# One core, a fused two-block transformer in split fp32: groups of TensorE transposes issued two at a time

## The chip, the core and the metric

The kernel runs on one core of one Trainium2 chip. The time is the device time of one execution, in microseconds. The engines of the core run side by side and meet through semaphores: TensorE (PE), VectorE (DVE), ScalarE (ACT), GpSimd (POOL) and SyncE (SP), which issues the DMAs.

## What is computed

The reference takes 256 tokens of width 2048 through three layers, all in fp32, and each weight is used once:

```python
# layer 0: stick-breaking attention, then the residual update; layer 1: latent attention, same update
x = x + rms_norm(out, g_post)
x = x + (p_i @ w_pp) * sigmoid(x @ w_pg)
# shared keys/values of layer 1
ckv, k_rope = split(rms_norm(x, kv_norm) @ w_dkv)
# last layer: 16 meta tokens in front; gated linear attention and causal pooling, side by side
q, k, v, r, glr, pu = split(rmsnorm(h, norm1) @ w_in)
h = h + concat(gla(q, k, v, glr) * silu(r), pool(pu)) @ w_out
h = h + square(relu(rmsnorm(h, norm2) @ mlp_w1)) @ mlp_w2      # 2048 -> 8192 -> 2048
```

## The kernel before, in words

**Units.** Every product streams its weight through a ring of four slots of 128 x 1024 elements. SP loads a unit into `raw` (L358, L414), ACT copies it rounded into `whi` (L1016), DVE writes the rest `raw - whi` into `wlo` (L1494), and PE takes three matmuls for each tile: hi times hi, hi times lo, lo times hi (L485, L486, L487; L852 to L854 in the last layer's transposed products; L961 and L964 in the MLP's up products). A unit has two k tiles of 512 columns: 2 x 2 token tiles x 3 = 12 matmuls. A chunk is 8 units, 96 matmuls, and gives 512 output columns for both token tiles. The `ckv` stage is narrower, 288 columns for each matmul, and the stages `k2`, `v2` and `pu` have 272.

**Lead.** `along` on ACT and on DVE runs through a chunk unit by unit: first the split of the unit that is three ahead (ACT waits until PE has used the slot's last unit), then the hooks of that unit.

**Transposes.** Activations are produced token by token and must lie channel by channel as the next product's left operand. They are turned on PE against the identity, in batches (`batch`, L497) of four 128 x 128 transposes that fill one PSUM bank `tp[n % 2]`. ACT then takes the bank as the hi part (`hi_batch`, L1049 without a gain, L1052 with one, L1035 for `mixed`), DVE the lo part (`lo_batch`, L1523 and L1527) and frees the bank with `tp_done`. Batch n waits in `batch` until batch n - 2 is done. Batches are numbered in one global order, `BATCH`. Each activation of width 2048 has 8 groups: `ogA` and `ogB` (gated attention outputs), `x1` and `x3` (residuals into the gate products), `x2a`, `x2b`, `x4` (residuals into the next layer), `mixed`, `x5`. `ckv` and `cq` (latents) have two each, `qdec` (decayed queries) 2, `kend` (keys) 2, `vT` (values) 4.

**Hooks.** A plan such as `{1: [3], 2: [4]}` says: ahead of unit 1 turn group 3, ahead of unit 2 group 4. PE, ACT and DVE each follow the same plan in their own streams: `turns` on PE, `his` on ACT, `los` on DVE. With `need=name`, unit u of a product waits until group u of that name is done. Where a turned group isn't hooked to a unit it stands between two chunks, as `x1` in the `ple` stage (one unit a chunk) of `post`.

**Attention of layer 1.** The stage `attb` runs head pairs in slots `c` = 0 to 7. In the last slot its four units stand with `ogB` turned ahead of units k = 1, 2, 3; `turned(c)` (L715) transposes the probabilities ahead of the last unit, ACT copies them (L1300), `outputs(c)` (L722 to L724) multiplies with the values, and ACT's `silu_out` (L1156) frees the accumulators for `out_b`, whose first product waits for it (`gates_out`).

Of the kernel before, what the change touches and what calls it, by code (L numbers as in the profile page):

```python
# [143 lines left out]
def build(nc, w, const, out):  # L144
# [3 lines left out]
    with ctx:  # L148
# [306 lines left out]
        def _(pe):  # L455
# [215 lines left out]
            product(S["cq"], 0, ahi, alo, need="x2b", hooks=join(turns_staged("ckv", {4: [0], 5: [1]}, c + 1, c), {7: [turn_k_rope]}))  # L671
# [61 lines left out]
            for c in range(SLOTS):  # L733
                more = c + 1 < SLOTS
                for k, (query, uu) in enumerate(slot_units(c)):
                    if k == 0:
                        scores(c)
                        if c == 0:
                            evacuated(S["uv2"].c0 + 1)
                        elif c % 2 == 0:  # L740
                            pe.wait_ge(evac_act, gate_chunk_at(c // 2 - 1) + 1)
                    if not more and k:
                        turn("ogB", k - 1)
                    if query and uu == 0 and c:
# [12 lines left out]
                outputs(c)  # L757
# [78 lines left out]
            def columns(name, j, hooks={}):  # L836
# [5 lines left out]
                for uu in range(s.units):  # L842
# [61 lines left out]
            product(S["r2"], 1, x4hi, x4lo, hooks=join({6: [heads_out]}, turns("mixed", {6: [0], 7: [1]})))  # L904
# [100 lines left out]
        def _(act):  # L1005
# [179 lines left out]
            def post(layer, y, x1, x2, gain, norms):  # L1185
                s = S[f"out_{'ab'[layer]}"]
                for j in range(4):
                    p = (s.c0 + j) % 2
                    along(s, j, his(y, bhi, None, OG_LATE if layer == 0 else SPREAD) if j == 0 else {})
# [13 lines left out]
                for j in range(4):  # L1203
                    p = (s.c0 + j) % 2
                    split_to(s.u0 + j + 4)
                    if j:
                        hi_batch(x1, j - 1, ahi)
                    ended(s, j)
                    for t in range(TT):
                        m = act.activation(pp[:, t, j * CH:(j + 1) * CH], acc[p][t][:, :], ACT.Copy)  # L1210
                    m.then_inc(evac_act, 1)
                s = S[f"gate{layer}"]
                for j in range(4):
# [5 lines left out]
                    hooks = join({4: [last_squares]}, his(x2, x4hi if layer else bhi, gain, ALONG[j])) if j else his(x1, ahi, None, SPREAD)  # L1219
# [37 lines left out]
            along(s, 0, his("ckv", kvhi, GC["kvl"], {4: [0], 5: [1]}))  # L1257
# [33 lines left out]
            for c in range(SLOTS):  # L1291
                for query, uu in slot_units(c):
                    if uu % 4 == 3:
                        if c:
                            act.wait_ge(sem("attB_out"), c)
                        if c == SLOTS - 1:
                            hi_batch("ogB", 1, bhi)
# [5 lines left out]
                    if c == SLOTS - 1 and uu % 4 == 1:  # L1303
                        hi_batch("ogB", 0, bhi)
# [9 lines left out]
                if c == SLOTS - 1:  # L1314
                    hi_batch("ogB", 2, bhi)
# [86 lines left out]
            for j in range(2):  # L1402
                p = (s.c0 + j) % 2
                along(s, j, join({0: [lambda: hi_pooled(3)]}, his_mixed({6: [0], 7: [1]})) if j else
# [82 lines left out]
        def _(dve):  # L1487
# [178 lines left out]
            def post(layer, y, x1, x2, gain, norms):  # L1666
                s = S[f"out_{'ab'[layer]}"]
                for j in range(4):
                    p = (s.c0 + j) % 2
                    along(s, j, los(y, bhi, blo, None, OG_LATE if layer == 0 else SPREAD) if j == 0 else {})  # L1670
# [13 lines left out]
                for j in range(4):  # L1684
# [4 lines left out]
                    if j >= 1:  # L1689
                        lo_batch(x1, j - 1, ahi, alo)  # L1690
                    split_to(s.u0 + j + 4)
                s = S[f"gate{layer}"]
                for j in range(4):
                    c, p = s.c0 + j, (s.c0 + j) % 2
                    hooks = los(x2, x4hi if layer else bhi, x4lo if layer else blo, gain, ALONG[j]) if j else los(x1, ahi, alo, None, SPREAD)
# [32 lines left out]
            along(s, 0, join(los("ckv", kvhi, kvlo, GC["kvl"], {4: [0], 5: [1]}), {7: [k_rope_out]}))  # L1728
# [66 lines left out]
            for c in range(SLOTS):  # L1795
                more = c + 1 < SLOTS
                scores_out(c)
                for k, (query, uu) in enumerate(slot_units(c)):
# [11 lines left out]
                    if not more and k in (1, 2):  # L1810
                        lo_batch("ogB", k - 1, bhi, blo)
                outputs_over_sums(c)
                if c == SLOTS - 1:
                    lo_batch("ogB", 2, bhi, blo)
# [83 lines left out]
            for j, hooks in enumerate(({1: [keys_from_start], 3: [keys_to_end]},  # L1898
                                       {0: [lambda: decayed_queries_out(0)], 1: [lambda: decayed_queries_out(1)],
                                        2: [lambda: turned_out("kend", 0, kend[:, 0, :])], 3: [lambda: turned_out("kend", 1, kend[:, 1, :])]},  # L1900
                                       {1: [lambda: values_turned(0)], 3: [lambda: values_turned(1)]}, {1: [lambda: values_turned(2)]})):
                columns("v2", j, vT[:, 2 * j, :], vT[:, 2 * j + 1, :], sem("vT"), hooks)
# [65 lines left out]
            for j, hooks in enumerate(({1: [lambda: values_turned(3), lambda: turned_out("kvM", 0, kvM[:, :])], 3: [lambda: head_in(0)]},  # L1968
# [6 lines left out]
                                   los("mixed", ahi, alo, mixed_gain, {6: [0], 7: [1]})))  # L1975
# [191 lines left out]
```

## Time and profile before

| | |
|---|---|
| Median of 3 runs | 2110.72 us (2108.91, 2110.72, 2110.99) |
| The profiled execution's own time | 2112.99 us |
| Its span, first to last instruction | 2111.2 us |
| PE busy in the span | 2095.2 us, 99% |
| DVE, ACT, POOL busy | 1209.6, 1047.9, 111.3 us |
| Granted TensorE clock, mean | 0.998 |
| Moved by DMA | 375.09 MB, 178 GB/s |

Busy time is the union of an engine's instructions. On PE the matmuls are pipelined: one of 512 columns is shown some 0.39 us long, and the next starts 0.23 us after it, so on PE the starts count, not the lengths. In a timeline row "x4" after an instruction means four of that kind in a row, the time is that from the first's start to the last's end, and "[0.54 <-ACT stg L1156]" is idle time ahead of it with what ended that.

### The profile page before, as it was taken

How to read it: one execution, taken by the hardware profiler on the slowest of the kernel's cores; microseconds unless marked ns; L12 is line 12 of the kernel's file. 1: busy time of each engine (PE TensorE's matmuls, PEld its weight loads, DVE VectorE, ACT ScalarE, POOL GpSimd, SP SyncE). 2: the span in 40 equal slices, each digit the busy share in tenths (PEclk: the TensorE clock that was granted, in tenths of full speed). 3: DMA queues.
4: the chain of work that ended last, by engine and by line, in shares of the span. 5: the costliest groups of instructions: out<-in, count | busy, mean ns of one | idle time of the engine just before them, and what ended most of it. 6: DMA issues, size and time to landing. Idle time of an engine off the chain costs nothing.

```text
span 2111.2 us, 26739 instructions
## 1 busy us (share of the span) xinstructions
PE 2095.2 (99%) x10740; PEld 1784.2 (85%) x10740; DVE 1209.6 (57%) x1371; ACT 1047.9 (50%) x1400; POOL 111.3 (5%) x98
## 2 busy tenths in 40 slices
PE   9999999999999999999999999999999999999998
PEld 7888887888898888888889998888888888888887
DVE  5555555556666556556655557556555655655655
ACT  6443566645565455445555345554434434534443
POOL 0000334100000121000000000000000000000000
PEclk9999999999999999999999999999999999999999
DMA  7666544555555544555554546556566566566654
GB/s 255 183 186 188 170 150 147 171 192 188 181 161 182 153 149 135 171 185 191 184 163 140 145 135 200 185 176 193 193 192 189 190 196 188 188 196 190 188 191 149
DMA packets 209052, 375.09 MB, mean 178 GB/s; under 512 B 13844, under 2 KB 44790, under 8 KB 208535
## 3 DMA queue, kind: packets, MB, share of 16 engines
q1 hardware_dynamic: 208934, 373.46, 56.7%
q8 instruction: 82, 1.34, 0.3%
q14 instruction: 36, 0.29, 0.0%
HBM read 371.31 MB, written 2.10 MB: 177 GB/s over the span
## 4 chain that ended last, share of the span: by engine, by line
PE 96%; ACT 1%; POOL 1%; DVE 1%; issue 0%; DMA 0%; SPq 0%; ACTq 0%; POOLq 0%
PE acc L485 22%; PE acc L487 22%; PE acc L486 22%; PE acc L961 6%; PE xb L961 3%; PE tp L961 3%; PE tp L497 3%; PE acc L964 3%; PE acc L852 2%; PE acc L853 2%; PE acc L854 2%; PE tp L964 1%; PE xb L964 1%; PE tp L600 1%; PE xb L706 0%; PE xb L707 0%
## 5 line engine op out<-in xcount | busy, mean ns | idle before, releaser
L1494 DVE TENSOR_TENSOR wlo<-raw,whi 128x1024 fp32r<-128x1024 f32 (+2 forms) x706 | 865.2, 1228 | 770.6 <-ACT whi L1016 769.5
L1016 ACT ACTIVATE whi<-raw 128x1024 fp32r<-128x1024 f32 (+2 forms) x706 | 737.1, 1046 | 857.7 <-PE acc L487 616.1
L485 PE MATMUL acc<-whi,ahi 128*128 128x512 f32 x1552 | 614.3, 396 | 0.0
L487 PE MATMUL acc<-whi,alo 128*128 128x512 f32 x1552 | 605.3, 390 | 0.0
L486 PE MATMUL acc<-wlo,ahi 128*128 128x512 f32 x1552 | 604.5, 390 | 0.0
L487 PEld LDWEIGHTS acc<-whi,alo 128*128 128x128 f32 x1552 | 291.3, 188 | 61.6
L486 PEld LDWEIGHTS acc<-wlo,ahi 128*128 128x128 f32 x1552 | 291.8, 188 | 57.7
L485 PEld LDWEIGHTS acc<-whi,ahi 128*128 128x128 f32 x1552 | 291.6, 188 | 57.5
L961 PE MATMUL acc<-bT,whi 128*128 128x512 f32 x512 | 161.3, 396 | 1.1 <-DVE x L1993 0.7
L485 PE MATMUL acc<-whi,bhi 128*128 128x512 f32 (+1 forms) x320 | 120.4, 376 | 0.5 <-ACT stg L1156 0.5
L487 PE MATMUL acc<-whi,blo 128*128 128x512 f32 (+1 forms) x320 | 118.6, 371 | 0.0
L486 PE MATMUL acc<-wlo,bhi 128*128 128x512 f32 (+1 forms) x320 | 118.5, 370 | 0.0
L964 PEld LDWEIGHTS acc<-bT,wlo 128*128 128x128 f32 x512 | 96.2, 188 | 22.7
L964 PE MATMUL acc<-bT,wlo 128*128 128x256 f32 x512 | 100.6, 278 | 0.0
L852 PE MATMUL acc<-lhi,whi 128*128 128x272 f32 x320 | 93.9, 294 | 0.0
L853 PE MATMUL acc<-llo,whi 128*128 128x272 f32 x320 | 93.2, 291 | 0.0
L854 PE MATMUL acc<-lhi,wlo 128*128 128x272 f32 x320 | 92.9, 290 | 0.0
L961 PE MATMUL tp<-bT,whi 128*128 128x512 f32 x256 | 80.4, 395 | 0.0
L961 PE MATMUL xb<-bT,whi 128*128 128x512 f32 x256 | 80.4, 395 | 0.0
L961 PEld LDWEIGHTS acc<-bT,whi 128*128 128x128 f32 x512 | 78.2, 189 | 2.2 <-DVE x L2036 1.0
L485 PEld LDWEIGHTS acc<-whi,bhi 128*128 128x128 f32 x320 | 60.1, 188 | 10.5 <-ACT stg L1156 0.7
L487 PEld LDWEIGHTS acc<-whi,blo 128*128 128x128 f32 x320 | 60.1, 188 | 10.2
(323 smaller groups left out, 2256.6 us busy)
## 6 DMA issues: line engine op xcount, KB each, us to landing
raw<-in_mlp_w SPq DMA_DIRECT2D x256, 512.0 KB, 4.3
raw<-in_w_in_a SPq DMA_DIRECT2D x128, 512.0 KB, 3.8
raw<-in_w_ple_gate SPq DMA_DIRECT2D x64, 512.0 KB, 3.9
raw<-in_w_in SPq DMA_DIRECT2D x64, 512.0 KB, 3.8
raw<-in_w_in_b SPq DMA_DIRECT2D x40, 512.0 KB, 3.6
raw<-in_w_out_a SPq DMA_DIRECT2D x32, 512.0 KB, 4.3
raw<-in_w_out_b SPq DMA_DIRECT2D x32, 512.0 KB, 4.3
raw<-in_w_out SPq DMA_DIRECT2D x32, 512.0 KB, 4.2
```

Of the source, the lines that this page charges most:

```text
L485: pe.matmul(o, hi[:, kt, tok], whi[:, slot, wc], start=start, stop=False)
L486: pe.matmul(o, hi[:, kt, tok], wlo[:, slot, wc], start=False, stop=False)
L487: mm = pe.matmul(o, lo[:, kt, tok], whi[:, slot, wc], start=False, stop=stop)
L497: mm = pe.transpose(tp[n % 2][:, o:o + k], src, ident[0:k, 0:k])
L600: pe.matmul(tp[i][:, 0:3 * P], const_of("suffix"), tA[:, i, :], start=True, stop=False)
L852: pe.matmul(o, whi[:, slot, wc], lhi[:, kt, :], start=first and k == 0, stop=False)
L853: pe.matmul(o, whi[:, slot, wc], llo[:, kt, :], start=False, stop=False)
L854: mm = pe.matmul(o, wlo[:, slot, wc], lhi[:, kt, :], start=False, stop=last and k == s.kt - 1)
L961: pe.matmul(banks[ct][:, :], whi[:, slot, wc[ct]], bT[:, kt, :, :].rearrange("p i t -> p (i t)"), start=first and k == 0, stop=False)
L964: mm = pe.matmul(banks[ct][:, 0:SEQ], wlo[:, slot, wc[ct]], x5hi[:, kt, :], start=False, stop=end)
L1016: act.activation(whi[:, u % RING, 0:n], raw[:, u % RING, 0:n], ACT.Copy).then_inc(hi_done, 1)
L1494: dve.tensor_tensor(wlo[:, u % RING, 0:n], raw[:, u % RING, 0:n], whi[:, u % RING, 0:n].bitcast(F32), ALU.subtract).then_inc(lo_done, 1)
```

## The change

Groups that were turned one at a time at successive units are turned two at a time, at every second unit. The plans change, and so do the places in the code where groups were turned without a plan. The same transposes are issued in the same order with the same copies behind them.

```diff
-LAST = {3: [6], 4: [7]}
-SPREAD = {1: [3], 2: [4], 3: [5], 4: [6], 5: [7]}
-OG_EARLY, OG_LATE = {5: [0], 6: [1], 7: [2]}, {0: [3], 1: [4], 2: [5], 3: [6], 4: [7]}
-EACH = {f: [f] for f in range(8)}
-MIXED_LATE = {1: [4], 2: [5], 3: [6], 4: [7]}
-ALONG = {1: {4: [0], 5: [1]}, 2: {4: [2], 5: [3]}, 3: {4: [4], 5: [5]}}
+LAST = {4: [6, 7]}
+EACH = {f: [f, f + 1] for f in range(0, 8, 2)}
+X1_LATE = {1: [4, 5], 3: [6, 7]}
+OG_EARLY, OG_LATE = {6: [0, 1]}, {0: [2, 3], 2: [4, 5], 4: [6, 7]}
+MIXED_EARLY, MIXED_LATE = {7: [0, 1]}, {1: [4, 5], 3: [6, 7]}
+ALONG = {1: {5: [0, 1]}, 2: {5: [2, 3]}, 3: {5: [4, 5]}}
...
@@ PE, post() @@
-                    product(S[f"out_{ab}"], j, bhi, blo, need=y if j == 0 else None, free=gates_out if layer and j == 0 else None, hooks=turns(y, OG_LATE if layer == 0 else SPREAD) if j == 0 else {})
+                    product(S[f"out_{ab}"], j, bhi, blo, need=y if j == 0 else None, free=gates_out if layer and j == 0 else None, hooks=turns(y, OG_LATE) if j == 0 else {})
...
                     product(S[f"ple{layer}"], j, phi[:, layer], plo[:, layer])
-                    if j:
-                        turn(x1, j - 1)
+                    if j % 2:
+                        for f in (j - 1, j):
+                            turn(x1, f)
...
-                    hooks = turns(x2, ALONG[j]) if j else turns(x1, SPREAD)
+                    hooks = turns(x2, ALONG[j]) if j else turns(x1, X1_LATE)
...
-            product(S["cq"], 0, ahi, alo, need="x2b", hooks=join(turns_staged("ckv", {4: [0], 5: [1]}, c + 1, c), {7: [turn_k_rope]}))
+            product(S["cq"], 0, ahi, alo, need="x2b", hooks=join(turns_staged("ckv", {5: [0, 1]}, c + 1, c), {7: [turn_k_rope]}))
...
@@ PE, last slot of attb @@
-                    if not more and k:
-                        turn("ogB", k - 1)
+                    if not more and k == 2:
+                        for f in range(2):
+                            turn("ogB", f)
...
@@ PE, last layer @@
-            columns("v2", 1, {0: [lambda: turn_decayed_queries(0)], 1: [lambda: turn_decayed_queries(1)],
-                              2: [lambda: turn_keys(0)], 3: [lambda: turn_keys(1)]})
-            columns("v2", 2, {1: [lambda: turn_values(0)], 3: [lambda: turn_values(1)]})
-            columns("v2", 3, {1: [lambda: turn_values(2)]})
+            columns("v2", 1, {1: [lambda f=f: turn_decayed_queries(f) for f in range(2)], 3: [lambda t=t: turn_keys(t) for t in range(TT)]})
+            columns("v2", 2, {2: [lambda h=h: turn_values(h) for h in range(2)]})
+            columns("v2", 3, {2: [lambda: turn_values(2)]})
...
-            product(S["r2"], 1, x4hi, x4lo, hooks=join({6: [heads_out]}, turns("mixed", {6: [0], 7: [1]})))
+            product(S["r2"], 1, x4hi, x4lo, hooks=join({6: [heads_out]}, turns("mixed", MIXED_EARLY)))
...
@@ ACT, units uu of slot c of attb @@
                         if c:
                             act.wait_ge(sem("attB_out"), c)
-                        if c == SLOTS - 1:
-                            hi_batch("ogB", 1, bhi)
...
                     split_to(u + 4)
                     u += 1
-                    if c == SLOTS - 1 and uu % 4 == 1:
-                        hi_batch("ogB", 0, bhi)
+                    if c == SLOTS - 1 and uu % 4 == 2:
+                        for f in range(2):
+                            hi_batch("ogB", f, bhi)
...
-                if c == SLOTS - 1:
-                    hi_batch("ogB", 2, bhi)
                 if c % 2:
                     act.wait_ge(unit_used, u)
                     silu_out(acc[1], 0, "pre1")
```

ACT's and DVE's other edits mirror these, plan for plan.

## Rows read from the trace of the kernel before

**Rows 1.** The page of the profile: busy time; then busy tenths in 40 slices.
```profile
PE 2095.2 (99%) x10740; PEld 1784.2 (85%) x10740; DVE 1209.6 (57%) x1371; ACT 1047.9 (50%) x1400; POOL 111.3 (5%) x98
...
PEclk9999999999999999999999999999999999999999
```

**Rows 2.** The waits of PE: waiting line, releaser, total us, times, longest.
```profile
PE acc L961 <- DVE x L1993: 0.7, 1, 0.7
PE acc L485 <- ACT stg L1156: 0.5, 1, 0.5
```

**Rows 3.** Timeline of PE in the `qk` stage, where two groups stand together.
```profile
49.21 1.03 PE L497 MATMUL tp<-tab,stg 128*128 128x128 f32 x8
50.00 0.48 PE L485 MATMUL acc<-whi,ahi 128*128 128x512 f32 x1
...
207.89 1.04 PE L497 MATMUL tp<-tab,stg 128*128 128x128 f32 x8
```

**Rows 4.** Timeline of PE, single groups in the first `gate` chunk, then one chunk each.
```profile
519.40 0.60 PE L497 MATMUL tp<-tab,x 128*128 128x128 f32 x4
519.75 0.48 PE L485 MATMUL acc<-whi,ahi 128*128 128x512 f32 x1
...
529.00 0.60 PE L497 MATMUL tp<-tab,x 128*128 128x128 f32 x4
...
548.53 0.60 PE L497 MATMUL tp<-tab,x 128*128 128x128 f32 x4
...
593.98 0.60 PE L497 MATMUL tp<-tab,x 128*128 128x128 f32 x4
```

**Rows 5.** Timeline of PE without transposes, 512 columns.
```profile
428.15 0.39 PE L485 MATMUL acc<-whi,bhi 128*128 128x512 f32 x1
...
436.31 0.39 PE L485 MATMUL acc<-whi,bhi 128*128 128x512 f32 x1
```

**Rows 6.** Timeline of PE in the second `ckv` chunk, 288 columns.
```profile
619.45 0.60 PE L497 MATMUL tp<-tab,x 128*128 128x128 f32 x4
...
620.28 0.29 PE L485 MATMUL acc<-whi,bhi 128*128 128x288 f32 x1
...
621.08 0.29 PE L485 MATMUL acc<-whi,bhi 128*128 128x288 f32 x1
...
633.67 0.60 PE L497 MATMUL tp<-tab,x 128*128 128x128 f32 x4
```

**Rows 7.** Timeline of ACT and of DVE behind the first of these.
```profile
620.68 0.83 ACT L1052 ACTIVATE ahi<-tp,gcol 128x256 fp32r<-128x256 f32 x2
...
621.54 0.88 DVE L1527 SCALAR_TENSOR_TENSOR alo<-tp,gcol,ahi 128x256 fp32r<-128x256 f32 x2
```

**Rows 8.** Timelines of PE, ACT and DVE ahead of the meta rows, 512 columns.
```profile
1060.22 0.60 PE L497 MATMUL tp<-tab,x 128*128 128x128 f32 x4
...
1063.51 1.17 PE L497 MATMUL tp<-tab,metax 16*128 16x16 f32 x16
...
1061.44 0.82 ACT L1052 ACTIVATE lhi<-tp,gcol 128x256 fp32r<-128x256 f32 x2
...
1062.72 0.87 DVE L1527 SCALAR_TENSOR_TENSOR llo<-tp,gcol,lhi 128x256 fp32r<-128x256 f32 x2
```

**Rows 9.** Timelines of PE and ACT from the last slot of `attb` into `out_b`.
```profile
874.34 0.50 PE L485 MATMUL acc<-whi,bhi 128*128 128x512 f32 x1 [0.54 <-ACT stg L1156]
...
871.11 0.60 ACT L1049 ACTIVATE bhi<-tp 128x512 fp32r<-128x512 f32 x1
871.73 1.28 ACT L1156 ACT_TABLE_LOAD   x1
873.02 1.26 ACT L1156 ACTIVATE stg<-acc,rs 128x512 f32<-128x512 f32 x2
```

**Rows 10.** Windows: PE, PEld, DVE, ACT, POOL busy; PEclk, DMA share, GB/s.
```profile
49.20:50.20 1.00, 1.00 (x10) 0.98 (x9) 0.00 (x0) 0.73 (x1) 0.00 (x0) 1.00 0.75 287
...
1104.20:1107.60 3.40, 3.40 (x16) 3.39 (x16) 0.00 (x0) 0.59 (x1) 0.00 (x0) 0.50 0.51 154
```

More of the change, by code:

```diff
@@ L1188, in post @@
                     p = (s.c0 + j) % 2
-                    along(s, j, his(y, bhi, None, OG_LATE if layer == 0 else SPREAD) if j == 0 else {})
+                    along(s, j, his(y, bhi, None, OG_LATE) if j == 0 else {})
                     ended(s, j)
@@ L1205, in post @@
                     split_to(s.u0 + j + 4)
-                    if j:
-                        hi_batch(x1, j - 1, ahi)
+                    if j % 2:
+                        for f in (j - 1, j):
+                            hi_batch(x1, f, ahi)
                     ended(s, j)
@@ L1218, in last_squares @@
                         squares(norms, j - 1, x)
-                    hooks = join({4: [last_squares]}, his(x2, x4hi if layer else bhi, gain, ALONG[j])) if j else his(x1, ahi, None, SPREAD)
+                    hooks = join({4: [last_squares]}, his(x2, x4hi if layer else bhi, gain, ALONG[j])) if j else his(x1, ahi, None, X1_LATE)
                     along(s, j, join(hooks, {6: [meta_in], 7: [meta_root]}) if layer and j == 3 else hooks)
@@ L1256, in _ @@
             p = s.c0 % 2
-            along(s, 0, his("ckv", kvhi, GC["kvl"], {4: [0], 5: [1]}))
+            along(s, 0, his("ckv", kvhi, GC["kvl"], {5: [0, 1]}))
             ended(s, 0)
@@ L1403, in _ @@
                 p = (s.c0 + j) % 2
-                along(s, j, join({0: [lambda: hi_pooled(3)]}, his_mixed({6: [0], 7: [1]})) if j else
+                along(s, j, join({0: [lambda: hi_pooled(3)]}, his_mixed(MIXED_EARLY)) if j else
                       {2 * g + 1: [lambda g=g: hi_pooled(g)] for g in range(3)})
@@ L1669, in post @@
                     p = (s.c0 + j) % 2
-                    along(s, j, los(y, bhi, blo, None, OG_LATE if layer == 0 else SPREAD) if j == 0 else {})
+                    along(s, j, los(y, bhi, blo, None, OG_LATE) if j == 0 else {})
                     ended(s, j)
@@ L1688, in post @@
                                                  in1=x[:, t, cols], op0=ALU.mult, op1=ALU.add).then_inc(done, 1)
-                    if j >= 1:
-                        lo_batch(x1, j - 1, ahi, alo)
+                    if j % 2:
+                        for f in (j - 1, j):
+                            lo_batch(x1, f, ahi, alo)
                     split_to(s.u0 + j + 4)
@@ L1694, in post @@
                     c, p = s.c0 + j, (s.c0 + j) % 2
-                    hooks = los(x2, x4hi if layer else bhi, x4lo if layer else blo, gain, ALONG[j]) if j else los(x1, ahi, alo, None, SPREAD)
+                    hooks = los(x2, x4hi if layer else bhi, x4lo if layer else blo, gain, ALONG[j]) if j else los(x1, ahi, alo, None, X1_LATE)
                     along(s, j, join(hooks, {6: [meta_in], 7: [meta_rs]}) if layer and j == 3 else hooks)
@@ L1727, in k_rope_out @@
                 dve.tensor_copy(krT[ROPE:P, 1, :], tp[n % 2][ROPE:P, 0:SEQ]).then_inc(tp_done, 1)
-            along(s, 0, join(los("ckv", kvhi, kvlo, GC["kvl"], {4: [0], 5: [1]}), {7: [k_rope_out]}))
+            along(s, 0, join(los("ckv", kvhi, kvlo, GC["kvl"], {5: [0, 1]}), {7: [k_rope_out]}))
             ended(s, 0)
@@ L1809, in _ @@
                         roped_out(c + 1)
-                    if not more and k in (1, 2):
-                        lo_batch("ogB", k - 1, bhi, blo)
+                    if not more and k == 2:
+                        for f in range(2):
+                            lo_batch("ogB", f, bhi, blo)
                 outputs_over_sums(c)
-                if c == SLOTS - 1:
-                    lo_batch("ogB", 2, bhi, blo)
                 if c % 2:
@@ L1898, in _ @@
             for j, hooks in enumerate(({1: [keys_from_start], 3: [keys_to_end]},
-                                       {0: [lambda: decayed_queries_out(0)], 1: [lambda: decayed_queries_out(1)],
-                                        2: [lambda: turned_out("kend", 0, kend[:, 0, :])], 3: [lambda: turned_out("kend", 1, kend[:, 1, :])]},
-                                       {1: [lambda: values_turned(0)], 3: [lambda: values_turned(1)]}, {1: [lambda: values_turned(2)]})):
+                                       {1: [lambda f=f: decayed_queries_out(f) for f in range(2)],
+                                        3: [lambda t=t: turned_out("kend", t, kend[:, t, :]) for t in range(TT)]},
+                                       {2: [lambda h=h: values_turned(h) for h in range(2)]}, {2: [lambda: values_turned(2)]})):
                 columns("v2", j, vT[:, 2 * j, :], vT[:, 2 * j + 1, :], sem("vT"), hooks)
@@ L1974, in _ @@
             along(S["r2"], 1, join({0: [lambda: lo_pooled(3)], 1: [lambda: heads_gated(0)]},
[L1975 removed]
+                                   los("mixed", ahi, alo, mixed_gain, MIXED_EARLY)))
             heads_gated(1)
```

## The prediction

> **What bounds the kernel now.** I read the page's busy times first: PE is busy for 2095.2 of 2111.2 us, DVE for 57%, ACT for 50%, and the clock row shows nines throughout [rows 1]. So the time is the length of PE's instruction stream and nothing else, as long as the others keep up. Then I read PE's waits, to see whether they do: the only waits outside the start of more than 0.5 us are one at the MLP's first product (0.7) and one for ACT's `stg`, which the page puts at 0.5 in all [rows 2]. That leaves two ways in which this change can act: a batch of transposes costs PE more or less than before, or a wait comes or goes. I read the timeline of PE where the old kernel already turns two groups together, and where it turns one.
>
> **What a single group and a pair cost PE.** Without transposes, 36 matmuls of 512 columns take 436.31 - 428.15 = 8.16 us, 0.2267 each, so a unit of 12 takes 2.72 [rows 5]. With a single group ahead of each unit, three units take 529.00 - 519.40 = 9.60, or 3.20 each: a single costs 0.48 us [rows 4]. Of that, 0.35 lies between the group's start and the next matmul's start; the rest is that this first matmul is followed late. In a pair the same distance is 50.00 - 49.21 = 0.79 [rows 3], so the second group adds 0.44 and a pair should cost 0.48 + 0.44 = 0.92, against 0.96 for two singles: 0.04 saved. The same from whole chunks: seven chunks of 96 matmuls and one pair take (207.89 - 49.21) / 7 = 22.669 each [rows 3], two chunks of 96 and two singles take (593.98 - 548.53) / 2 = 22.725 each [rows 4]: 0.056 saved. The two ways differ because small irregularities of the matmuls behind a group differ. I take 0.05 for each pair at 512 columns, with 0.04 and 0.056 as bounds. What is saved is the passage from transposes to matmuls and back, not the transposes.
>
> At 288 columns it is another matter. Six bare matmuls take 621.08 - 620.28 = 0.80, a unit 1.60; seven units with a single take (633.67 - 619.45) / 7 = 2.03 [rows 6]. A single costs 0.43 to 0.44, which is what the second group of a pair costs anyway, so merging saves nothing here. The row of the second group is at 512 columns; at 288 none stands. Bounds: 0 and, by the wide ones, 0.05. I take 0, and the same for the 272 columns of `v2`, which lie nearest to these.
>
> **How many pairs.** Four each for `ogA`, `x1`, `x2a`, `x2b`, `ogB`, `x3`, `x4` and `x5` (32), one each for `ckv`, `qdec`, `kend` and `vT`, three more for `mixed` (its groups 2 and 3 stood together already): 39 new pairs. `ogB` saves three passages only, since its third group stood directly ahead of `turned`, in one run of transposes with it. So 38 passages go. Narrow are `x2b`'s four, the last of `x2a` (its `LAST` lies in `ckv`), and `qdec`, `kend`, `vT`: 8. Wide: 30, the last of `x5`, among the up product's matmuls of two widths, counted in. 30 x 0.05 = 1.5 us (1.2 to 1.7), and 8 x 0 (0 to 0.4).
>
> **The wait that goes.** In the last slot of `attb`, ACT takes `ogB`'s group 2 between its split and the table load for `silu_out`: 871.11, then 871.73, then `stg` to 874.28; PE sits idle for 0.54 us and starts `out_b` at 874.34 [rows 9]. In the new order ACT has no hi batch after this split: the table load comes 0.5 to 0.6 us nearer to it, at 0.60 for the batch less the overlap of its start. What is late next is PE itself: `silu_out` also waits for the last unit's end, which allows it some 0.1 us more or less than the table load does, and then needs 1.26 for two tiles, while PE has the six matmul pairs of `outputs` to do, 1.3 us. So the wait shrinks from 0.54 to about 0.1. I take 0.45 (0 to 0.54). The group itself isn't saved: it is turned at the first unit of `out_b`, and is in the count above.
>
> **The waits that could come.** Batch n waits until batch n - 2 is done. With singles one unit apart it had two units and a group for that. The first of a pair has two units and a group of its predecessor pair, and so has the second: 6.3 us at 512 columns. Work behind a wide group with a gain: turned at 1060.22, hi until 1062.26, lo until 1063.59, 3.4 us [rows 8]. The second of a pair follows on ACT and DVE by one more batch of 0.82 to 0.88 [rows 8], counted from the pair's start 4.2 us, against 0.44 + 6.3. That is hidden with 2 us to spare, and since `along` does a unit's split first, a pair delays the next split by 0.9 us on engines that are half idle; the queue behind them is the ring, three units ahead. DMAs stay as they are: SP waits for `lo_done`, at most 0.9 us later, on loads that have two units left. Four places are tighter.
> - `x2b` in the second `ckv` chunk. The first pair is turned at 619.45; ACT's hi batches would run 620.68 to 621.51 and to 622.3, DVE's lo from 621.54 to 622.42 and to 623.3 [rows 7]. The next pair's second group comes at 619.45 + 0.88 + 2 x 1.60 + 0.44 = 623.97. 0.6 us to spare; if the pair of `x2a` before it pushes ACT's norm chain by half a batch, 0.2.
> - The meta rows, turned one unit after the last `x4` pair of the gate product: 0.88 + 2.72 = 3.60 us after its start, with 3.4 us of work behind its first group [rows 8]. 0.2 to spare.
> - `x1` and `x3` between the `ple` chunks: pairs 3.6 us apart at their closest (the one ahead of `gate`, and unit 1). Without a gain a batch is 0.6 on ACT [rows 9], and the split doesn't go ahead of it; I estimate the second group done after 3 us, and 4.0 are allowed.
> - `mixed` group 5 behind group 3: the existing pair is turned, and the new one now stands one unit behind it, with its second group needing group 3. By the sum above, less the split of 1 us, which doesn't go ahead of it here, 3.2 against 0.88 + 2.72 + 0.44 = 4.04.
> I count these waits as 0 (0 to 1 us together).
>
> **The sum.** -1.5 - 0 - 0.45 + 0 = -1.95 us. On the profiled execution, 2112.99 becomes 2111.0 (span 2111.2 to 2109.3). That execution lay 2.3 above the median of the runs, so the median 2110.72 becomes 2108.8, 0.09% less. A change of 0.2%, 4.2 us, is about what a measurement can tell from none here; the runs of before alone spread over 2.1.
>
> **The rivals.**
> - Nothing from the passages: the irregularities that make 0.04 and 0.056 differ eat the rest, or the tight places above cost what the pairs save. Then 2110.3 to 2111. For it: the gain of a pair is a tenth of one group, and the two workings disagree by a third. Against it: seven chunks repeat it. Chance 0.13.
> - Slower: the wait for bank n - 2 moves to the second group of the pairs, because hi and lo batches come doubled while the splits ahead of them don't. It needs the second group to be late by 2.0 us more than nothing in all before the kernel is slower at all, and by 6.2 in all, 0.16 at each of 39 pairs, before it shows: ACT and DVE would have to lag their present place by over 2 us [rows 8]. At 0.2 a pair the time is 2108.8 + 7.8 = 2116.6. Against it: DVE at 57%, no wait of PE for a lo batch now [rows 1, 2]. Chance 0.04.
> - The clock falls at pairs. [...] Chance 0.01. [...]
> - [...] Chance 0.09, of which most is still within 0.2%.
>
> **How the numbers follow.** The sum as forecast has 0.73, with 2107.2 to 2110.3 by its bounds and a scatter of 1 us between medians. The range reaches to the others on both sides: down to 2106.6, up to 2111.3, and holds 8 in 10 or more. Faster by over 0.2% means below 2106.5: 0.07, from the last rival and scatter. Slower by over 0.2%: 0.05, the second and third rivals. Same: 0.88.
>
> **What would show it.** In the trace after: rows "x8" for the transposes, 0.79 to the next matmul's start; a gate chunk of 22.67 where 22.73 stood; a `ckv` chunk of unchanged length; no or a 0.1 us wait ahead of `out_b`; no wait of PE for `lo_batch`. Wrong would be: waits "PE tp L497 <- DVE" in PE's waits, a clock row below nine in the middle, or a gate chunk of unchanged length.

## The result and the profile after

The kernel after takes 2108.84 us in the median of 20 runs (2106.84 to 2110.19), the kernel before 2111.13 (20 runs, 2108.91 to 2113.36). The medians differ by 2.29 us, 0.11%; the ratio over all the runs is put at 0.9984, 95% interval 0.9978 to 0.9990. That is too little to be told from no change at the 0.2% set ahead, though the interval leaves 1 out. The profiled execution took 2108.89 us, its span 2107.1, where before had 2112.99 and 2111.2.

The page of the kernel after, busy time and clock. PE is busy for 3.2 us less and still for 99%:

```profile
PE 2092.0 (99%) x10740; PEld 1784.0 (85%) x10740; DVE 1207.7 (57%) x1371; ACT 1047.8 (50%) x1400; POOL 111.3 (5%) x98
...
PEclk9999999999999999999999999999999999999999
```

The waits of PE after (waiting line, releaser, total us, times, longest). ACT's `stg` [rows 2] has no row any more, and none for a lo batch (`DVE alo`, `blo`, `llo`) has come:

```profile
PE tp L600 <- POOL tA L2110: 1.9, 2, 1.2
PE tp L497 <- DMA x<-in_x: 0.8, 1, 0.8
PE acc L962 <- DVE x L1992: 0.7, 1, 0.7
PE tp L497 <- POOL roped L2089: 0.4, 2, 0.2
```

The timeline of PE after, one pair in each of three `gate` chunks. From pair to pair it is 22.65 and 22.69 us, 45.34 for two chunks, where two with two singles each took 45.45 [rows 4]:

```profile
550.29 1.03 PE L497 MATMUL tp<-tab,x 128*128 128x128 f32 x8
551.08 0.48 PE L485 MATMUL acc<-whi,ahi 128*128 128x512 f32 x1
...
572.94 1.04 PE L497 MATMUL tp<-tab,x 128*128 128x128 f32 x8
573.73 0.47 PE L485 MATMUL acc<-whi,ahi 128*128 128x512 f32 x1
...
595.63 1.03 PE L497 MATMUL tp<-tab,x 128*128 128x128 f32 x8
```

PE, and below it ACT, after, from the last slot of `attb` into `out_b`. ACT's table load follows the split at once and `silu_out` is done at 872.14. `product` waits for it before it runs its hooks, so it is the pair of `ogB` that waits now: it begins at 872.19, 0.13 us behind the end of `outputs` (871.67 + 0.39 = 872.06), where `out_b` had waited 0.54 [rows 9]. A wait as short as this gets no bracket in a timeline and no row in the waits:

```profile
871.67 0.39 PE L725 MATMUL acc<-vB,pB 128*128 128x128 f32 x2
872.19 1.09 PE L497 MATMUL tp<-tab,nat 128*128 128x128 f32 x8
873.04 0.48 PE L485 MATMUL acc<-whi,bhi 128*128 128x512 f32 x1
```

```profile
868.50 1.06 ACT L1017 ACTIVATE whi<-raw 128x1024 fp32r<-128x1024 f32 x1
869.58 1.28 ACT L1157 ACT_TABLE_LOAD   x1
870.88 1.26 ACT L1157 ACTIVATE stg<-acc,rs 128x512 f32<-128x512 f32 x2
```

**Where the 4.1 us of the two profiled executions lie.** The kernels issue the same matmuls in the same order. So I took, in both traces, the starts of matmuls with equally many matmuls and transposes ahead of them, and followed how the distance between the two grows. By place, in us:

```
ogA, 4 passages                          -0.254
x1, 4                                    -0.174
x2a, the 3 wide ones                     -0.187
x2a's last and x2b, 5 narrow             -0.034
ckv, 1                                   -0.060
attb, no passage                         +0.054
ogB: into out_b 1, behind it 2           -0.597 -0.136
x3, 4                                    -0.173
x4, 4                                    -0.147
between 1100 and 1112, no passage        -1.487
qdec, kend, vT, 3 narrow                 -0.040
mixed, 3                                 -0.134
x5, 4                                    -0.219
other small steps                        +0.034
sum                                      -3.554
```

How fine this is can be read from two executions of one kernel, the kernel after and its repetition in the fifth experiment: they agree within 0.03 us at every place that was edited, but differ by up to 0.07 in a stretch of `attb` and by 0.16 over the whole program behind the start. So the places hold to some hundredths, and the sum to some tenths.

The remaining half microsecond lies ahead of the first of these places, in the start of the program, where `x` arrives earlier (0.8 us of waiting above, 1.36 in the trace of before). Two parts of the 4.1 are thus no work of the pairs themselves: the start, and the 1.487 us at 1100 to 1112. There the kernel before had 3.4 us of half clock behind the gate logits [rows 10]; in the kernel after the windows over the logits and behind them (us; PE, PEld, DVE, ACT, POOL busy; PEclk, DMA share, GB/s) show full clock:

```profile
1099.00:1102.00 3.00, 3.00 (x9) 0.80 (x7) 1.23 (x1) 2.19 (x3) 0.00 (x0) 1.00 0.00 0
1101.90:1105.30 3.40, 3.40 (x27) 3.33 (x27) 0.00 (x0) 0.59 (x1) 0.00 (x0) 1.00 0.53 154
```

The change proper is -3.554 + 1.487 = -2.07 us by this pair of traces. The experiments ask three things: is each term of it what it was taken for, what would a bank wait have cost, and whose are the 1.49 us and the start.

### The profile page after: what moved, and what is told of

The parts are those of the page before. It is cut to its first block, busy times and chain, and to the rows that moved or that the text cites. A ratio compares the mean times of both kernels' runs of the same rounds, so it can differ in the third digit from the quotient of the medians.

```text
span 2107.1 us, 26740 instructions
## 1 busy us (share of the span) xinstructions
PE 2092.0 (99%) x10740; PEld 1784.0 (85%) x10740; DVE 1207.7 (57%) x1371; ACT 1047.8 (50%) x1400; POOL 111.3 (5%) x98
## 4 chain that ended last, share of the span: by engine, by line
PE 96%; ACT 1%; POOL 1%; DVE 1%; issue 0%; DMA 0%; SPq 0%; ACTq 0%; POOLq 0%
PE acc L485 22%; PE acc L487 22%; PE acc L486 22%; PE acc L962 6%; PE tp L962 3%; PE xb L962 3%; PE tp L497 3%; PE acc L965 3%; PE acc L854 2%; PE acc L855 2%; PE acc L856 2%; PE xb L965 1%; PE tp L965 1%; PE tp L600 1%; PE xb L707 0%; PE xb L708 0%
```

## The experiments

The first four have one run each, with one of the kernel before at 2112.88 beside them. Their totals say little, since the clock's fall alone moves them by 1.5 us; the distances between traces, taken as above, say more.

### Only ogB in pairs

The kernel before with the new order of `ogB` and nothing else:

```diff
+OGB_LATE = {0: [2, 3], 2: [4, 5], 4: [6, 7]}
-                    if not more and k:
-                        turn("ogB", k - 1)
+                    if not more and k == 2:
+                        for f in range(2):
+                            turn("ogB", f)
```

> The kernel before with the edits of ogB alone: its groups in pairs in the last attention slot and in out_b. Read on the trace, at matmuls of equal number with equally many transposes ahead of them. My theory (passages plus one wait): three passages of 0.05 us and a wait of ACT's stg ahead of out_b that shrinks from 0.54 us idle by 0.4 to 0.5, 0.55 to 0.75 us in all, and nothing anywhere else. Rival (all of the gain is passages, the wait is late elsewhere instead): 0.15 us, with the wait of 0.5 still there or moved behind out_b's first unit.

Measured: 2112.35, span 2110.6. Against before the trace is level to 0.014 us until 860, then -0.598 and -0.136 by 905, and level again to the end. It has the fall of the clock. The ACT timeline and PE's:

```profile
870.82 1.28 ACT L1158 ACT_TABLE_LOAD   x1
872.12 1.26 ACT L1158 ACTIVATE stg<-acc,rs 128x512 f32<-128x512 f32 x2
```

```profile
872.91 0.39 PE L725 MATMUL acc<-vB,pB 128*128 128x128 f32 x2
873.43 1.09 PE L498 MATMUL tp<-tab,nat 128*128 128x128 f32 x8
874.28 0.48 PE L486 MATMUL acc<-whi,bhi 128*128 128x512 f32 x1
```

With this order alone the idle time goes from 0.54 us to 0.13 (872.91 + 0.39 = 873.30, and the pair begins at 873.43, behind `stg` at 873.38). The table load starts 0.91 us sooner than in the kernel before (870.82, 871.73), but PE's own stream is 0.50 ahead at `outputs`, since the group that stood ahead of `turned` is turned later; the wait shrinks by the difference, 0.41. The 0.734 us are 3 passages at 0.05, 0.41 of idle time, and 0.17 beside them. Some 0.1 of that can be read: `out_b`'s first matmul was followed after 0.34 us instead of 0.23 already in the kernel before, without transposes ahead of it, and is followed after 0.32 with the pair there, so that this pair pays next to nothing for it. The rest stays open.

### Only the narrow pairs

`x2b`, `qdec`, `kend` and `vT` in pairs, the rest as before:

```diff
-EACH = {f: [f] for f in range(8)}
+EACH = {f: [f, f + 1] for f in range(0, 8, 2)}
```

and the three plans of `v2` from the diff of the change.

> The kernel before with pairs only where the matmuls are narrow: x2b in the second ckv chunk (288 columns) and qdec, kend, vT in v2 (272 columns); seven passages fewer. My theory (the passage costs only where the matmul behind it is 512 wide): 0 to 0.1 us on the trace in all, no wait of PE for a lo batch, the second ckv chunk as long as before (2.03 us a unit, 4.06 for two). Rival (every passage costs the same 0.05): 0.35 us.

Measured: 2111.88. In `ckv` -0.035 for four passages, at `v2` -0.020 for three: 0.008 each. PE's timeline in the second `ckv` chunk:

```profile
619.72 1.04 PE L497 MATMUL tp<-tab,x 128*128 128x128 f32 x8
...
631.88 1.04 PE L497 MATMUL tp<-tab,x 128*128 128x128 f32 x8
```

Three periods of a pair take 12.16, 4.053 each; two periods of a single were 2 x 2.03 [rows 6]. A narrow passage is worth nothing to speak of. No wait for a lo batch stands in PE's waits, so the place with 0.2 to 0.6 us to spare held. This execution had no fall of the clock (-1.487 at the gate logits) though its logits are those of before.

### The old pairs made singles

The other direction: the eight pairs that the kernel before already had in `qk` are split over units 4 and 5.

```diff
-turns_staged("qk", {4: [12, 13]}, 6)
+turns_staged("qk", {4: [12], 5: [13]}, 6)
```

> The kernel before with the edit turned round where it had pairs: the eight pairs of the qk stage are split into single groups at two successive units. My theory (0.05 us for each passage at 512 columns, whatever the stage): 8 x 0.05 = 0.4 us longer on the trace, chunks of 22.72 us where 22.67 stood. Rival (the shorter chunks of qk come from the stage, not from the pair): chunks stay at 22.67, 0 us.

Measured: 2111.55, and +0.479 us by the end of `qk` for eight passages more, 0.060 each; no other place moves but the fall of the clock, which this execution doesn't have. PE's timeline:

```profile
48.77 0.60 PE L497 MATMUL tp<-tab,stg 128*128 128x128 f32 x4
49.13 0.48 PE L485 MATMUL acc<-whi,ahi 128*128 128x512 f32 x1
...
51.97 0.60 PE L497 MATMUL tp<-tab,stg 128*128 128x128 f32 x4
```

So among 512-column matmuls the price is that of a passage and not of one stage.

### Pairs too close together

The kernel after with `x2b`'s pairs at units 0, 1, 2, 3 instead of 0, 2, 4, 6. This makes the wait that the second rival supposes.

```diff
-EACH = {f: [f, f + 1] for f in range(0, 8, 2)}
+EACH = {f // 2: [f, f + 1] for f in range(0, 8, 2)}
```

> The changed kernel with the four pairs of x2b in the second ckv chunk ahead of units 0, 1, 2, 3 instead of 0, 2, 4, 6, so that two units' lead becomes one. My theory (batch n waits for batch n - 2, which is done 2.9 and 3.8 us after its pair's start, and the next pair would stand only 0.88 + 1.60 us behind): each of the three later pairs waits 0.4 to 1.4 us, 1.5 to 4 us in all, PE waits for DVE's lo batch ahead of L497. Rival (the lead doesn't matter, ACT and DVE catch up within a unit): under 0.3 us.

Measured: 2110.42. PE's waits have a new row, and its timeline shows the pair torn in two:

```profile
PE tp L497 <- DVE alo L1526: 0.9, 3, 0.6
```

```profile
616.62 1.03 PE L497 MATMUL tp<-tab,x 128*128 128x128 f32 x8
617.41 0.38 PE L485 MATMUL acc<-whi,bhi 128*128 128x288 f32 x1
...
618.95 0.29 PE L487 MATMUL acc<-whi,blo 128*128 128x288 f32 x1
619.86 0.63 PE L497 MATMUL tp<-tab,x 128*128 128x128 f32 x4 [0.61 <-DVE alo L1526]
620.64 0.63 PE L497 MATMUL tp<-tab,x 128*128 128x128 f32 x4 [0.16 <-DVE alo L1526]
621.02 0.38 PE L485 MATMUL acc<-whi,bhi 128*128 128x288 f32 x1
...
625.12 0.29 PE L487 MATMUL acc<-whi,blo 128*128 128x288 f32 x1
625.43 0.63 PE L497 MATMUL tp<-tab,x 128*128 128x128 f32 x4
626.21 0.63 PE L497 MATMUL tp<-tab,x 128*128 128x128 f32 x4 [0.15 <-DVE alo L1526]
626.59 0.38 PE L485 MATMUL acc<-whi,bhi 128*128 128x288 f32 x1
```

By the distance to the kernel after it costs 1.77 us within the chunk, as much as 35 passages at 512 columns. The waits named make 0.9 of it, since they count from the shown end of a matmul, which lies behind the start of the next. By the starts the rows have nearly all of it: 0.91 and 0.31 us from the last matmul to the torn pairs where 0.13 is usual (0.78 and 0.18 lost), 1.16 from a torn pair's start to its product where the first pair has 0.79 (0.37 twice), and 0.09 at the pair between them. So the bank wait is real, and it is the unit between two pairs that keeps it away.

### The gate logits in three parts, after and before

In both profiled kernels the gate logits are six thin matmuls (33 rows) in one run of 3 us. Now two each stand ahead of units 1, 2 and 3.

```diff
-            columns("k2", 0, {1: [gate_logits]})
+            columns("k2", 0, {t + 1: [lambda t=t: gate_logits(t)] for t in range(TT + 1)})
```

> The kernel after, with one edit: the six matmuls of the gate logits (33 rows, 3.0 us in one run behind unit 0 of k2) stand in three parts of two, ahead of units 1, 2 and 3. Theory: it is this run of thin matmuls that lets the clock fall to half behind it in some executions and not in others (in the profile before it did, 3.4 us and 1.49 us lost by the level of the matmuls behind; in the profile after it did not). Spread, each part is 1.0 us between full matmuls and the clock never falls: no half-clock stretch at 1104 in the profile, the median 0 to 0.7 us under that of the kernel after in the same call, and no run above 2109.6. Rival 1: the fall has nothing to do with the thin matmuls; then it is as frequent as before, and the highest runs stand at 2110.2 or above. Rival 2: two more passages between thin and full matmuls cost 0.05 each or more, and the median rises by 0.1 to 0.5.

> The same edit of the gate logits on the kernel before. Theory: the kernel before loses 1.49 us in the executions in which the clock falls there, so its highest runs (2112.7 to 2113.4) go, none stands above 2111.5, and the median goes from 2111 to 2109.2 to 2111.0; the distance to the kernel with the edit and pairs is then the change proper, 2.07 us. Rival: the high runs stay, median 2111.1 and up.

> The kernel after, unchanged, for its place beside the others of this call. Expected: median 2108.8 with runs near 2107.0, 2108.9 and, seldom, 2110.2; ratio to the kernel before 0.9984 to 0.9992, 0.9990 being the change proper (2.07 us) where the clock falls equally often in both.

Measured: the kernel after unchanged 2108.85 (11 runs, 2106.94 to 2109.74), with its logits in parts 2109.73 (2107.36 to 2110.70). On the kernel before 2112.21 (2111.08 to 2113.53, and one of 2993 left out), where before itself has 2111.22 in 33 runs. PE's timeline, in parts:

```profile
1099.54 1.12 PE L795 MATMUL tp<-gw,glrT 33*128 33x512 f32 x2
1100.59 0.39 PE L855 MATMUL acc<-lhi,whi 128*128 128x272 f32 x1
...
1103.81 1.12 PE L795 MATMUL tp<-gw,glrT 33*128 33x512 f32 x2
```

and in the kernel after, in one run:

```profile
1099.10 1.98 PE L794 MATMUL tp<-gw,glrT 33*128 33x512 f32 x4
1101.02 1.03 PE L794 MATMUL xb<-gw,glrT 33*16 33x512 f32 x2
1101.97 0.39 PE L854 MATMUL acc<-lhi,whi 128*128 128x272 f32 x1
```

The distance to the kernel after grows by 0.60 us there, 0.30 for each of the two further parts. Rival 2 is right, and its upper bound was too low: a passage between these matmuls and the product costs six times what one of transposes does at 512 columns, though the matmuls behind have 272 here, where one of transposes cost 0.008. The logit matmuls differ from the product's in rows, in columns and in number format; which of these costs is not shown. Neither profile has the clock fall, but neither have five of the other profiles. The theory's bounds, no run above 2109.6 or 2111.5, both failed; but they left out the 0.60 us that the parts cost, so they don't decide by themselves whether the clock still falls. On the kernel before the rival's median, 2111.1 and up, is what came.

### Filling transposes between the first two groups

At the start PE runs 22 transposes of the identity ahead of the first product, behind the two groups of `x0`. Five of them are put between these groups, where PE waits for `x`:

```diff
-            for f in range(2):
-                turn("x0", f)
-            fill(22)
+            turn("x0", 0)
+            fill(5)
+            turn("x0", 1)
+            fill(17)
```

> The kernel after, with five of the 22 filling transposes at the start moved into the wait between the two groups of x0. Theory: the other 1.5 to 2 us by which executions differ come from the start, where the clock rises early in one (22 filling transposes take 2.56 us) and late in another (4.0 us); without PE's idle 0.8 to 1.9 us in that wait it rises early more often: the first product starts at 10.4 to 11.0 us instead of 12.1, and the median is 2107.0 to 2108. Rival: the clock rises at times that PE's idle time there does not decide; then the median stays at 2108.8, or rises by up to 0.5 us where x arrives before the five are through, and the start is spread as before.

Measured: 2106.77 (11 runs, 2106.49 to 2108.53), 2.08 us under the kernel after beside it, and more than the theory's 2107.0 to 2108 asked for; the first product starts earlier than its 10.4 to 11.0 too. PE's timeline of the kernel after:

```profile
7.43 1.11 PE L497 MATMUL tp<-tab,x 128*128 128x128 f32 x4 [0.81 <-DMA x<-in_x]
8.34 3.98 PE L553 MATMUL xb<-tab 128*128 128x128 f32 x22
12.07 0.48 PE L485 MATMUL acc<-whi,ahi 128*128 128x512 f32 x1
```

of another execution of it, where `x` came a little sooner:

```profile
7.17 0.66 PE L497 MATMUL tp<-tab,x 128*128 128x128 f32 x4 [0.58 <-DMA x<-in_x]
7.66 2.56 PE L553 MATMUL xb<-tab 128*128 128x128 f32 x22
9.98 0.48 PE L485 MATMUL acc<-whi,ahi 128*128 128x512 f32 x1
```

and with the five moved:

```profile
6.42 0.73 PE L553 MATMUL xb<-tab 128*128 128x128 f32 x5
7.64 0.66 PE L497 MATMUL tp<-tab,x 128*128 128x128 f32 x4 [0.50 <-DMA x<-in_x]
8.14 2.02 PE L553 MATMUL xb<-tab 128*128 128x128 f32 x17
9.91 0.47 PE L485 MATMUL acc<-whi,ahi 128*128 128x512 f32 x1
```

The same 22 transposes take 3.98 us in one and 2.56 in the other: the clock rises in the midst of the first (the trace's record of it begins at 11.2 on the page) and ahead of the second. With the five moved, part of the wait for `x` is filled; the clock rises before 8.1 us in all four profiles taken with this edit (here and in the next experiment), and the first product starts at 9.7 to 10.0 us instead of 12.1. Of the ten profiles without the edit two have such an early rise. The runs now stand in two heaps, seven at 2106.49 to 2107.03 and three at 2108.23 to 2108.53, one between them.

### The same edit on the kernel before, and with both edits

With the start steadier the change can be measured with less scatter. The kernel before with the moved five, the kernel after with them and with the logits in parts, and the kernel after with them once more:

> The kernel before with the edit of the start alone (five of the 22 filling transposes between the two groups of x0). The kernel after with this edit ran at 2106.77, in two heaps: seven runs at 2106.5 to 2107.0, four at 2107.6 to 2108.5. With the start out of the way the change stands alone. Theory: it is worth 2.0 to 2.1 us (38 passages, and the wait ahead of out_b), so this kernel's lower heap stands at 2108.6 to 2109.1, and the upper one 1.5 us above; median 2108.9 where most runs are in the lower. Rival 1: the early clock depends on where the program's start falls and the edit had luck in one call: the median is 2111 as ever. Rival 2: the change also makes the fall at the gate logits rarer: then more than half of the runs here are in the upper heap, at 2110.3, against 4 of 11 with the pairs.

> The kernel after with both edits, of the start and of the gate logits. The gate logits in three parts cost 0.60 us by the profile (0.09 for the first, 0.51 for the two others), so the lower heap stands at 2107.1 to 2107.6. Theory: in three parts the clock no longer falls behind them; then there is no upper heap, and the 11 runs lie within 0.8 us. Rival: the fall doesn't need them in one run; then about a third of the runs stands at 2108.7 to 2109.2.

> The kernel after with the edit of the start, once more, beside the others of this call. Theory: median 2106.8, lower heap 2106.5 to 2107.0, some three or four of 11 runs at 2108.2 to 2108.6. Rival: where the edit only had luck in one call, the median is 2108.8.

Measured, 11 runs each: before with the edit 2109.43 (2108.70 to 2112.60), after with it 2107.51 (2106.60 to 2108.61), with both edits 2107.80 (2107.06 to 2110.09). The kernel before came out above the forecast 2108.9, and the kernel after above its 2106.8. With the runs of the experiment before it the kernel after with the edit has 22, median 2107.27. So the pairs are worth 2109.43 - 2107.27 = 2.16 us by the medians, or 1.92 by the two sets of 11 measured together; with runs in heaps such medians are loose, and by the means it is 2.50. The two profiles of this pair of kernels, both with the fall of the clock, are 2.30 apart behind the start, of which 0.17 lies in `attb`, where nothing was edited. All of it is near the 2.07 above, and none of it is finer than some tenths. In the kernel before four or five of 11 runs stand in an upper heap (2110.13 to 2110.58, and 2112.60), in the kernel after seven of 22 (2108.20 to 2108.61): from so few runs no difference, and rival 2 is not borne out.

The profile of the last kernel, at 2108.26, is of a run in its upper heap, and has the fall of the clock; the profile in the lower heap, at 2106.66, has 1.00 over the same 3.4 us. Windows behind the logits, of the first:

```profile
1100.30:1103.70 3.40, 3.40 (x18) 3.40 (x17) 0.00 (x0) 0.20 (x1) 0.00 (x0) 0.50 0.52 154
```

With both edits five runs lie at 2107.06 to 2107.30, as forecast for the cost of the parts, three at 2107.80 to 2108.24, and three at 2109.73 to 2110.09, 2.6 above the first. The theory's "within 0.8" fell, and so did the rival's 2108.7 to 2109.2. No profile was taken of such a run; what makes them is open, and that parts keep the clock up is not shown.

### The logits one unit later

Ten of the profiles so far have the logits in one run. The distance from the clock's rise at the start, as the trace records it, to the first logit matmul, in us:

```
clock falls behind them    1088.93  1089.16  1089.44  1092.14  1092.91
it does not                1087.88  1089.89  1090.06  1090.40  1090.69
```

The kernel before stood at 1089.44, the kernel after at 1087.88. The two rows don't overlap, though neither is one stretch. In the five profiles with the fall it came 1092.27 us (three) or 1095.68 us (two) behind the rise, to the hundredth and whatever the kernel. So in these five it kept to two distances from the rise, 1092.27 and 1095.68, while the logits stood between 1088.93 and 1092.91. The last experiment moves nothing but the logits, and ACT's work on them with them:

```diff
-            columns("k2", 0, {1: [gate_logits]})
+            columns("k2", 0, {2: [gate_logits]})
```

> The kernel before, with the six matmuls of the gate logits one unit (1.5 us) later, ahead of unit 2 of k2; nothing else. In ten profiles with the logits in one run, the distance from the clock's rise at the start to the first of them was 1088.93, 1089.16, 1089.44, 1092.14 or 1092.91 us where the clock fell behind them, and 1087.88, 1089.89, 1090.06, 1090.40 or 1090.69 where it did not. Of 80 runs of the kernel before, 33 lie above 2112.3, of 31 of the kernel after one lies above 2110.0. Theory: whether the clock falls is decided by where the logits stand against the clock's rise, and the change made the fall rarer only by bringing them 0.7 to 1.9 us nearer. Moved by 1.5 us here, they stand at 1090.7 to 1091.0 in the executions with a late rise that fell before: the heap above 2112.3 is gone or holds one of 11 runs, and the median is 2110.7 or less; the kernel before in the same call keeps its third or more up there. Rival: the fall comes by chance, or from the thin matmuls wherever they stand: then 3 to 6 of 11 runs are above 2112.3, and the median is that of the kernel before.

Measured: 2112.85 (11 runs, 2110.92 to 2113.77), nine of them above 2112.3; of the kernel before beside it 4 of 15 (median 2111.03), and 37 of all its 95. My distance was wrong: a unit of `k2` with all its matmuls is 3.2 us, not 1.5 (from the first part of the logits to the second it is 4.27 above, of which they take 1.05). So the logits stand at 1092.19 in its profile, beside 1092.14 and 1092.91, where the clock had fallen, and it fell again, 1095.68 us behind the rise. Windows over the logits and over the half clock:

```profile
1104.70:1107.50 2.80, 2.80 (x7) 0.71 (x6) 1.23 (x1) 2.19 (x3) 0.00 (x0) 1.00 0.62 187
1108.10:1111.50 3.40, 3.40 (x18) 3.40 (x17) 0.00 (x0) 0.10 (x1) 0.00 (x0) 0.50 0.50 154
```

The forecast of my theory, an empty upper heap, missed. But the rival of mere chance missed too, with 3 to 6 of 11 forecast and 9 found: with everything else equal (the two traces are level to 0.1 us otherwise) the place of the logits alone changes how many runs stand above 2112.3, where those profiled have the fall, from 4 of 15 to 9 of 11.

## Why the prediction was right

The forecast was 2108.8 us; 2108.84 came. Step by step:

- **The waits of PE are short.** The reading overlooked one row: PE waits twice for POOL's `tA` at L600, 1.2 us and 0.65, at 344 and 366 us and so not in the start. It did no harm here, since the row is 1.9 us in both kernels.
- **A passage at 512 columns saves 0.05 (0.04 to 0.056).** Right: 27 of them outside `ogB` measure 1.348 us, 0.050 each, from 0.037 at `x4` to 0.064 at `ogA`; the old pairs of `qk`, taken apart, give 0.060 each. With `ogB`'s three the term is 1.50, as forecast.
- **At 288 and 272 columns it saves nothing.** Right: 0.074 for eight in the change, 0.055 for seven alone, 0.008 to 0.009 each.
- **The wait ahead of `out_b` shrinks by 0.45.** Right in place and cause, and nearly in size: the idle time goes from 0.54 to 0.13, 0.41 less, and the 0.1 that was left over is there, now ahead of the pair. The place gives more than its two terms, 0.73 where 0.15 and 0.41 make 0.56; the 0.17 beside them stood in no term.
- **The waits that could come count 0.** Right at all four tight places: PE has no wait for a lo batch, and ahead of `x2b`'s pairs not even one too short for the views. The closest, the `ckv` chunk, holds with two units between pairs and breaks with one, at 1.77 us.
- **The sum.** 2.07 against 1.95, the difference being 0.13 more ahead of `out_b` (0.41 and 0.17 for 0.45), the 0.07 of the narrow passages and some 0.08 of small steps the other way, most of it in `attb`, where nothing was edited.
- **The clock does not fall at pairs.** Right. In the profile after the window 11.30:2103.50, in which all 39 new pairs stand, has a clock of 1.00, with PE busy for 2084.2 of 2092.2 us. The new pairs are eight transposes in a run; the change has no longer ones to show.
- **The last rival, more than the sum,** happened in the profiled execution and in part in the runs. The half-clock stretch of before (3.4 us at a clock of 0.50 [rows 10]) was absent, for 1.49 us. No run shows 1.7 us for it, half of 3.4: the matmuls of 272 columns start 0.227 apart there instead of 0.126, and by distances between traces the fall cost 1.48 to 1.53. Over all runs the mean went from 2111.47 (95) to 2108.48 (31), 2.99 us, 0.9 more than the change proper. Of the kernel before 37 of 95 runs stand above 2112.3, of the kernel after one of 31 above 2110.0, where that heap would be: 0.36 x 1.49 = 0.5 of the 0.9. By the times of the profiled executions, and so by my estimate, that heap holds only runs with a late rise and the fall (before: rise at 11.9 us, 2112.99); one with an early rise and the fall, as the profile of the kernel before with the moved five (rise at 6.7 us, logits at 1092.14, 2110.58), stands among the middle ones, where times can't tell it. The lowest runs have moved too, which by the one profile of such a run (the kernel after unchanged at 2106.94, rise at 6.4) have an early rise and no fall: up to 2109.9 us in the kernel before, 10 of 95, and up to 2107.3 in the kernel after, 9 of 31. The likely reason is that the pairs bring the logits nearer to the clock's rise, out of the distances at which it falls; that their place matters is shown by the last experiment (4 of 15 runs above 2112.3, and 9 of 11), that it does so for the change itself is only argued. The rest of the 0.9 isn't assigned.

That the median came out at the forecast to 0.04 us is in part luck. The kernel before has its median at 2111.03 over 95 runs, 0.3 above the three runs that the sum started from, and the medians moved 2.2 us (2.29 in the first 20 runs of each) where 1.95 was said; the two errors nearly cancel.

The kernel after with five filling transposes moved, median 2107.27 in 22 runs (ratios to before 0.9980, interval 0.9971 to 0.9989, and 0.9981, 0.9972 to 0.9990), is under both kernels. The edit at the start is worth 2108.85 - 2107.27 = 1.6 us by the medians, three quarters of what all 39 pairs are.

## What to carry to other kernels

Where PE is the bound, cost a transpose group by what it does to the matmul behind it: merging groups saved the passage alone here, 0.05 us at 512 columns and 0.01 at 272 or 288, so it pays only by number. Before merging, add up for each pair the copies behind it against the time until its bank is wanted again; the one place brought too close cost 1.77 us, 35 times what a merger saves at 512 columns. And where runs of one kernel stand in heaps, look for what makes the heaps before measuring a change of 0.1%. Here the kernel after ran at 2106.84 to 2110.19 (31 runs), and with five filling transposes moved at 2106.49 to 2108.61 (22 runs): a spread of 3.3 us and one of 2.1. Of the second kernel there are two profiles, one in the lower heap (2106.66) and one in the upper (2108.26). Over 1100.30 to 1103.70 us the first has a clock of 1.00 and the second one of 0.50, and by the distance between the two traces the second loses 1.51 of the 1.60 us there. The four runs between the heaps (2107.50 to 2107.63) have no profile.

## What the runs showed of the hardware

- Behind the six thin fp32 matmuls of the gate logits the clock stood at 0.50 for 3.4 us in six profiles, of eleven with the logits in one run; by the distance to profiles without it that cost 1.48 to 1.53 us. PE was busy ahead of it: over the logits for 3.00 of 3.00 us in the kernel before (1101.20:1104.20, weight loads 0.78) and for 2.80 of 2.80 with them one unit later (loads 0.71). In the kernel after, with no fall, it is 3.00 of 3.00 as well, with loads for 0.80, and the clock of 1.00 goes on for the 3.4 us behind. What makes it fall is not shown.
- The clock's rise at the start, as the trace records it, varies from one execution of a kernel to another: 11.2 us and 6.4 in two of the kernel after, 6.4 and 8.0 in two of the kernel after with the moved five, of which the second had the fall and the first had not.
- The fall came or stayed away with the distance from the rise to the first logit matmul, and not steadily: 1087.9 no, 1088.9 to 1089.4 yes, 1089.9 to 1090.7 no, 1092.1 to 1092.9 yes (us, eleven profiles). The fall itself came 1092.27 us behind the rise in three profiles and 1095.68 in the other three. With the logits one unit later and nothing else changed 9 of 11 runs stood above 2112.3, of the kernel before beside them 4 of 15.
- At the start, transposes whose results nobody reads, moved into PE's wait for `x`, won 1.6 us (medians 2108.85 and 2107.27): 22 transposes take 3.98 us where the clock rises among them and 2.56 where it has risen. The rise was early (6.2 to 8.0 us) in all four profiles with the edit and in two of ten without it (6.2 and 6.4, the others 11.2 to 12.4); what decides between the two without it isn't shown.
- A passage from a part of the thin logit matmuls (33 rows, 512 columns) to the product of 272 columns and back costs 0.30 us, six times one with transposes at 512 columns.
